# Levels of a block inverse: the turned inverse updated by a product of its own

## The reference

```python
decay = jnp.exp(jnp.where(causal, gc[..., :, None] - gc[..., None, :], -jnp.inf))
kb = k * beta[..., None]
a_in = jnp.einsum("bhnid,bhnjd->bhnij", kb, k) * decay
lmat = jnp.where(strict, a_in, 0.0) + jnp.eye(CHUNK, dtype=a_in.dtype)
rhs = jnp.concatenate([v * beta[..., None], kb * jnp.exp(gc)[..., None]], axis=-1)
sol = lax.linalg.triangular_solve(lmat, rhs, left_side=True, lower=True, unit_diagonal=True)
...
def step(state, xs):
    u_i, w_i, qk_i, q_i, k_i, gl = xs
    v_new = u_i - jnp.einsum("bhcd,bhde->bhce", w_i, state)
    o = jnp.einsum("bhcd,bhde->bhce", q_i, state) + jnp.einsum("bhij,bhje->bhie", qk_i, v_new)
    state = state * gl[..., None, None] + jnp.einsum("bhcd,bhce->bhde", k_i, v_new)
    return state, o
```

## Time and profile before

| | us |
|---|---|
| median of 3 runs | 2876.02 |
| lowest, highest | 2869.96, 2877.52 |
| profiled execution, whole | 2876.17 |
| its span, first to last instruction | 2874.4 |

### The profile page before, as it was taken

The page is one execution under the profiler, slowest core; times in us unless marked ns, Lnnn a source line. Parts: engine busy times, 40 slices in busy tenths (PEclk is TensorE's granted clock), DMA queues, the critical chain, the costliest instruction groups (busy, mean ns, idle before and its releaser), DMA issues.

```text
span 2874.4 us, 33482 instructions
## 1 busy us (share of the span) xinstructions
PE 2632.7 (92%) x13627; PEld 2108.3 (73%) x13638; DVE 1239.2 (43%) x1941; ACT 920.7 (32%) x1584; POOL 120.1 (4%) x156
## 2 busy tenths in 40 slices
PE   7999979997989988799999998888997899799997
PEld 6888868884544777678888786777785688688886
DVE  3434224116583233433332474433355441577722
ACT  3222223322345322232222334334334232333321
POOL 0000000000123000000000000122200000000000
PEclk9999988997699999989999898898997789799998
DMA  4333323220000223313333232000031022133331
GB/s 126 96 96 103 98 82 96 78 63 1 0 1 1 77 78 86 94 50 98 102 104 95 57 99 60 1 2 1 21 84 44 18 77 81 30 99 99 94 99 42
DMA packets 366280, 189.13 MB, mean 66 GB/s; under 512 B 11312, under 2 KB 363696, under 8 KB 366128
## 3 DMA queue, kind: packets, MB, share of 16 engines
q1 hardware_dynamic: 366128, 187.00, 22.9%
HBM read 184.87 MB, written 2.10 MB: 65 GB/s over the span
## 4 chain that ended last, share of the span: by engine, by line
PE 85%; DVE 9%; ACT 3%; issue 1%; POOL 1%; DMA 0%; SPq 0%; DVEq 0%; ACTq 0%
PE ps L396 22%; PE ps L397 22%; PE ps L398 22%; PE ps L439 3%; PE ps L558 2%; PE ps L790 2%; PE ps L826 1%; PE ps L577 1%; PE ps L450 1%; DVE pair_b L463 1%; PE ps L1452 1%; PE ps L795 1%; PE ps L698 1%; PE ps L1248 1%; PE ps L1243 1%
## 5 line engine op out<-in xcount | busy, mean ns | idle before, releaser
L396 PE MATMUL ps<-u_hi,w_hi 128*128 128x512 f32 (+1 forms) x2032 | 804.6, 396 | 50.0 <-DVE o_lo L930 20.7
L397 PE MATMUL ps<-u_lo,w_hi 128*128 128x512 f32 (+1 forms) x2032 | 799.1, 393 | 0.0
L398 PE MATMUL ps<-u_hi,w_lo 128*128 128x512 f32 (+1 forms) x2032 | 798.5, 393 | 0.0
L351 DVE TENSOR_TENSOR w_lo<-w_raw,w_hi 128x1024 fp32r<-128x1024 f32 (+2 forms) x366 | 417.9, 1159 | 434.7 <-ACT w_hi L367 420.4
L396 PEld LDWEIGHTS ps<-u_hi,w_hi 128*128 128x128 f32 (+1 forms) x2032 | 383.1, 189 | 147.6 <-DVE o_lo L930 21.8
L398 PEld LDWEIGHTS ps<-u_hi,w_lo 128*128 128x128 f32 (+1 forms) x2032 | 382.6, 188 | 85.3 <-issue 0.8
L397 PEld LDWEIGHTS ps<-u_lo,w_hi 128*128 128x128 f32 (+1 forms) x2032 | 383.5, 189 | 82.8 <-issue 0.9
L367 ACT ACTIVATE w_hi<-w_raw 128x1024 fp32r<-128x1024 f32 (+2 forms) x366 | 366.3, 1002 | 227.1 <-PE ps L398 226.3
L398 PE MATMUL ps<-mid_hi,w_lo 128*128 128x512 f32 x528 | 208.6, 395 | 0.0
L396 PE MATMUL ps<-mid_hi,w_hi 128*128 128x512 f32 x528 | 208.6, 395 | 0.0
L397 PE MATMUL ps<-mid_lo,w_hi 128*128 128x512 f32 x528 | 208.5, 395 | 0.0
(11 more groups left out here) (346 smaller groups left out, 2913.2 us busy)
## 6 DMA issues: line engine op xcount, KB each, us to landing
w_raw<-w_in_dram SPq DMA_DIRECT2D x101, 512.0 KB, 3.8
w_raw<-ffn_w_gate_dram SPq DMA_DIRECT2D x44, 512.0 KB, 4.9
w_raw<-ffn_w_up_dram SPq DMA_DIRECT2D x44, 512.0 KB, 3.9
w_raw<-w_up_dram SPq DMA_DIRECT2D x44, 512.0 KB, 3.8
w_raw<-ffn_w_down_dram SPq DMA_DIRECT2D x32, 512.0 KB, 3.9
w_raw<-w_out_dram SPq DMA_DIRECT2D x24, 512.0 KB, 4.0
w_raw<-w_down_dram SPq DMA_DIRECT2D x16, 512.0 KB, 3.8
w_raw<-ffn_w_down_dram SPq DMA_DIRECT2D x16, 384.0 KB, 3.5
```

The lines of the kernel that those rows point to most:

```text
L351: dve.tensor_tensor(lo, raw, hi.bitcast(F32), ALU.subtract).then_inc(w_split, 1)
L396: pe.matmul(out, wh, h_k, start=k0 + k == 0, stop=False)
L397: pe.matmul(out, wh, l_k, start=False, stop=False)
L398: mm = pe.matmul(out, wl, h_k, start=False, stop=end)
```

## The change

The turned matrix is no longer made from the new `upper`. Since the new `upper` is `upper` - X' `upper`, the new `Tm` is `Tm` - `upper`' X with the old `upper`. So stage "t" multiplies the old `upper` (as weights) with X, and needs no difference first; DVE subtracts the result from `Tm` (the new L1357), waits for that, and then does its other difference. ACT's turned copy is gone. The next level's "x" waits for DVE instead of ACT; level 0 still waits for ACT's t0.

```diff
-    ACT_STAGES = ["dec", "small", "t0"] + [x for x in lev if x[0] != "u"] + ["w"] + ...
+    ACT_STAGES = ["dec", "small", "t0"] + [("x", l) for l in range(NL)] + ["w"] + ...
...
             elif what == "x" and stage[1] == NL - 1:
-                pe.wait_ge(g_act, after("act", ("t", NL - 2), n))
+                pe.wait_ge(g_dve, after("dve", ("u", NL - 2), n))
...
                 pe.wait_ge(g_pool, after("pool", ("c", l), n))
-                pe.wait_ge(g_act, after("act", ("t", l - 1) if l else "t0", n))
+                if l:
+                    pe.wait_ge(g_dve, after("dve", ("u", l - 1), n))
+                else:
+                    pe.wait_ge(g_act, after("act", "t0", n))
...
             elif what == "t":
-                pe.wait_ge(g_dve, after("dve", ("u", stage[1]), n))
                 for c in range(QB):
                     for b in range(2):
-                        mm = pe.matmul(tile64(B[1], 0, b, c), tile64(upper(n), 0, b, c), ident[HALVES[b], HALVES[b]], start=True, stop=True)
+                        mm = pe.matmul(tile64(B[1], 0, b, c), tile64(upper(n), 0, b, c), tile64(X, 0, b, c), start=True, stop=True)
...
-            elif what == "t":
-                act.wait_ge(g_pe, after("pe", stage, n))
-                x = act.activation(Tm[:, 0:256], B[1][:, 0:256], ACT.Copy)
...
             elif what == "u":
-                dve.wait_ge(g_pe, after("pe", stage, n))
+                dve.wait_ge(g_pe, after("pe", ("t", stage[1]), n))
+                st.done(dve.tensor_tensor(Tm[:, 0:256], Tm[:, 0:256], B[1][:, 0:256], ALU.subtract))
                 x = dve.tensor_tensor(upper(n)[:, 0:256], upper(n)[:, 0:256], B[2][:, 0:256], ALU.subtract)
```

More of the change, by code:

```diff
@@ L1131, in build @@
     PE_STAGES = ["bc", "kk", "t0"] + lev + ["w"] + scan + ["ss", "bk"]
-    ACT_STAGES = ["dec", "small", "t0"] + [x for x in lev if x[0] != "u"] + ["w"] + [("v", c) for c in range(QB)] + ["sq", "rt"]
+    ACT_STAGES = ["dec", "small", "t0"] + [("x", l) for l in range(NL)] + ["w"] + [("v", c) for c in range(QB)] + ["sq", "rt"]
     DVE_STAGES = ["kb", "at", "qk"] + [("u", l) for l in range(NL - 1)] + ["full", ("u", NL - 1)] + [("s", c) for c in range(QB)] + ["inv", "out"]
```

## The result

The changed kernel takes 2885.88 us (median of 6 runs, 2884.89 to 2886.97) against 2874.64 us of the kernel before in the same comparison (6 runs, 2869.96 to 2877.52). The ratio is 1.0041 with an interval of 1.0028 to 1.0054; a second comparison, 5 runs against 9, gave 1.0035 (1.0022 to 1.0049). Slower by 0.4%, where 2888.6 us was forecast. The profiled execution has a span of 2883.1 us.

A forecast was written before the change was run, and what follows sets the result against it. Each head's chain of products and evictions was taken as the bound, not a full TensorE. Four transitions at 0.65 us plus 0.5 in the last, 3.1 per pair, 12.4 in all, added to 2876.2 gave 2888.6 us; range 2880 to 2896.

The forecast's parts named there:

- The bound: In the levels, each head is bound by its own chain of three products and three evictions, 3.68 us; TensorE is not full.
- The way round: From the second head's X copy to its next, through both heads' differences on DVE: 4.33 us per level against 3.68.
- rival C: In the levels, TensorE's clock drops to half: 2895 us with one level per pair, 34 us for all; 6% above 2894.
- the signs: Profile after: new difference 0.42 us, DVE busy up 17 us, ACT down 15, TensorE idle before X 0.5 and 0.2.
- The last transition: From the second head's last X copy to w: 4.87 us instead of 4.36, 0.5 us more per pair.
- The sum: Over the stage: 2.6 us from four transitions plus 0.5 from the last, 3.1 us per pair, 12.4 us for four pairs.
- A: In the levels, the heads do not hinder each other: 3.43 us per level instead of 3.68, 2871 us in total; 6%.
- B: In the levels, only the first head's way round binds, 3.90 us: 0.22 us more per level, 2880.6 us in total; 8%.
- the ring: Longest way round from one level's instruction to the next level's; with the new difference made twice it forecast 2908 us.
- D: Pairs fall into step with the clock's changes, or differences are a little slower: 2889 to 2894 us; 80% together with the forecast.

The follow-up runs named there:

- Staggered: "both" with the first head's next X product ahead of the second head's "u" product on TensorE: 2857.6 us, ratio 0.9944 to the kernel before.
- DVE copy: The kernel before with the turned copy made by DVE instead of ACT, nothing else: 2880.8 us, ratio 1.0021 to the kernel before.
- no turned difference: The changed kernel without the new difference L1357 and its wait: 2872.1 us, ratio 0.9990 to the kernel before.
- both: "early X" with each head's turned product ahead of its "u" product, one head after the other on TensorE: 2865.3 us, ratio 0.9965 to the kernel before.
- head order: The changed kernel with each head's turned product directly behind its "u" product on TensorE: 2872.8 us, ratio 0.9991 to the kernel before.
- early X: The changed kernel with both heads' turned differences first on DVE, X waiting for its turned difference alone: 2873.4 us, ratio 0.9987 to the kernel before.
- DVE order: The changed kernel with both heads' turned differences first on DVE, X still waiting for both of its head: 2892.1 us, ratio 1.0051 to the kernel before.
- double difference: The changed kernel with the turned difference L1357 made twice, first into an unused buffer part: 2920.9 us, ratio 1.0155 to the kernel before.

## Why the prediction was right

**The bound.** The step that mattered was reading the levels as two chains of product and eviction, not as a full TensorE, although the windows showed 10.88 of 11.00 us busy. "Staggered" shows what a full TensorE is: the same six stages in 2.80 us. "DVE copy" and "no turned difference" moved the level by what the chain said, with the same number of products in each.

**The way round.** Forecast 4.33 us per level, measured 4.35. The differences on DVE were put at 0.42 and 0.45 and were that; TensorE's idle time before X was put at 0.8 us per level in rival C and at 0.5 and 0.2 for the two heads among the signs; it was 0.67 and 0.23. The groups show 14.4 us for the full X products after a difference and 3.3 for the half-size ones, 17.7 us over 20 transitions, 0.89 each. Nothing waits in front of the turned product.

**The last transition.** Forecast 0.5 us more. From the end of the second head's last full-size X copy to w it was 4.36 us before and is 4.91 after (1875.91 to 1880.82), 0.55 more. The value was right, but one step of it was not. The sum had DVE take the first head's last "u" product at 4.40, with the copies of "full" over at 4.3; in fact the copies, which end at 4.36, are what it waits for:

```profile
1879.05 1.22 DVE L1350 COPY solve_t<-qkv 64x256 f32<-64x256 f32 x4
1880.30 0.42 DVE L1354 TENSOR_SCALAR solve_t<-ps 64x256 f32<-64x256 f32 x1
```

The product's last record had ended at 1880.04, 0.26 us before that difference started, where 0.11 is usual between the two. The two ways are that close here, so the right size of this term is in part luck; it is the same place that cost "both" 4 us. The copies ran at 288 ns since POOL had ended, as the sum had it: 284 to 292 ns for all 16, against 285 to 1046 before. That is as the Trainium skill ("SBUF — State Buffer", SBUF: two separate sides) has it for the port pair shared by DVE and GpSimd, and in "both", where POOL was not done when the copies began, the first of them took 0.72 us again. DVE's busy time went up by 11.4 us and not by the 17 named among the signs, since the copies took 5.3 us less; ACT's went down by 14.8.

**The sum.** Forecast 3.1 us per pair, measured 3.2 in the first and 3.35 in the others. The extra is in their first transition: the half-rate stretch reaches further into the first level there (5.3 us between a head's first two X copies instead of 5.19). The stage as a whole took 13.1 us more in place of 12.4. The part behind gave 3.3 us back in this trace and the part ahead 1.0, neither of which was in the forecast: 2888.6 + 0.7 - 3.3 - 1.0 = 2885.0, and the profiled run took 2884.9. So the mechanism was right, and the total is as near as it is because these errors are small and two of opposite sign; all are well inside the range.

**The rivals.** A (3.43 us per level, the heads out of each other's way) had its condition right, that the second head's X product does not wait behind the other head's differences. The change does not meet it, nor does "head order"; "early X" does, and took 3.45 us. Of the 5 us that A gave its stage kept nothing (203.9 us): first levels at half clock and the way to w took them. B (3.90 us) did not occur. C, the clock in the levels, did not occur at 79% busy; with one more difference per head it did, at some 13 us above the 2908 of the ring. D, that the pairs fall into step with the clock, looked right from this result: pairs 2 to 4 lie 58.01 us apart, and "head order" (54.5 to 54.6), "DVE order" (58.0 to 58.1) and "staggered" (51.1 to 51.3) are nearly even too. "Both" and "early X", with unequal distances, show that it is no general rule.

## What to carry to other kernels

In a stage that two chains share, write down the rings, through data and through each engine's order, and take the longest; a wait moved to an instruction that needs more than one result puts all of them on the ring. Signal a result as soon as the next step can use it: the same instructions took 4.35 us per level in one order and with one signal, 2.80 in another with two. Busy time of pipelined products does not show such slack; the distance between stages that follow each other without a wait does.

Follow the ring to its exit as well. Work that costs next to nothing beside a slow chain (here four copies on DVE ahead of the last difference) becomes the wait once the chain is fast.

## What the runs showed of the hardware

- Eight 64x64 products in fp32 (16 records) hold TensorE for 0.47 us at 2.4 GHz, 0.22 us being the passage of each. A stage that had to wait moves the end of the chain by 0.68 us.
- In the changed kernel's levels TensorE paused for at most 0.68 us at a time and was busy 10.37 of 13.10 us; the granted clock stayed at 1.00. In "double difference" it paused for 0.7 to 1.1 us at a time, and windows with 1.40 of 3.20 and 1.67 of 3.30 us busy were followed by windows at 0.51 and 0.50, though no pause was over 1.12 us.
- What a faster stretch gains can be taken or given elsewhere by the granted clock. In "early X" a level took 0.24 us less than in the kernel before, and 3.8 us went in first levels that ran longer at 1.2 GHz; the changed kernel got 3.2 us back over 200 us behind its last changed instruction. For differences of a few tenths of a percent the trace has to be cut at the borders of the stage before a total is explained.
